# Two 64-column operands side by side for the level scores and the router, and slots counted by token halves

## What is computed

```python
def step(state, xs):                      # chunks of the recurrence, four heads
    qc, kc, vc, gc = xs
    b = jnp.cumsum(gc, axis=-2)
    diff = b[:, :, :, None, :] - b[:, :, None, :, :]
    decay = jnp.exp(jnp.where(causal[:, :, None], diff, -jnp.inf))
    scores = jnp.einsum('bhtk,bhsk,bhtsk->bhts', qc, kc, decay)
...
def hierarchical_moe(h, w_rg, w_re, w_gate, w_up, w_down):
    g_logits = (t @ w_rg).astype(F32)     # 4 groups
    e_logits = (t @ w_re)...              # 16 experts, those of the best group are kept
    top_v, top_i = lax.top_k(e_in, TOP_K_IN_GROUP)
    act = (jax.nn.silu(hg) * hu * gates[..., None])
    y = jnp.einsum('nef,efd->nd', act, w_down)
```

## Time and profile before

| what | value |
|---|---|
| median of 3 runs | 1021.76 us (1020.68 to 1021.91) |
| the profiled execution | 1021.73 us, of which the span is 1019.8 us |
| PE busy | 999.2 us (98%) |
| PE weight loads busy | 547.1 us (54%) |
| DVE busy | 477.2 us (47%) |
| ACT, POOL busy | 136.4 us, 98.8 us |
| read from HBM | 283.33 MB |
| products of the levels (L715) | 256 matmuls in the trace, 31.2 us |
| products of the router (L926) | 64 matmuls, 7.5 us |

### The profile page before, as it was taken

One profiled execution on the slowest core, in us unless ns is written; L12 is line 12 of the kernel. 1 busy time (PEld: TensorE's weight loads), 2 busy tenths in 40 slices (PEclk: granted clock), 3 DMA queues, 4 the chain that ended last, 5 costly groups with the idle time before them and its releaser, 6 DMA issues.

```text
span 1019.8 us, 11159 instructions
## 1 busy us (share of the span) xinstructions
PE 999.2 (98%) x4494; PEld 547.1 (54%) x4494; DVE 477.2 (47%) x814; ACT 136.4 (13%) x323; POOL 98.8 (10%) x123
## 2 busy tenths in 40 slices
PE   8999999999999999999999999999999999999996
PEld 7657555669575454333334855565975433333332
DVE  2533375766554224432444636566655544444424
ACT  2211000411010010101112000032120010111111
POOL 3051032000010000000000512210000100000000
PEclk9999999999999999999999999999999999999999
DMA  9973000963379999999999420067385799999995
GB/s 359 425 299 131 35 0 6 409 249 123 125 277 391 406 423 421 419 423 420 421 420 420 163 82 1 1 254 285 148 327 193 297 421 420 421 420 421 421 415 220
DMA packets 44826, 293.58 MB, mean 288 GB/s; under 512 B 5472, under 2 KB 5728, under 8 KB 13024
## 3 DMA queue, kind: packets, MB, share of 16 engines
q1 hardware_dynamic: 38000, 266.36, 64.3%
q10 hardware_dynamic: 5616, 22.24, 5.6%
q0 software_dynamic: 1152, 4.19, 1.1%
HBM read 283.33 MB, written 9.44 MB: 287 GB/s over the span
## 4 chain that ended last, share of the span: by engine, by line
PE 89%; SPq 5%; DMA 3%; DVE 2%; issue 1%; POOL 0%; ACT 0%; DVEq 0%; POOLq 0%
PE bank L1001 18%; PE bank L1075 10%; PE bank L590 8%; PE bank L620 6%; PE bank L789 5%; PE bank L622 5%; PE bank L600 5%; PE bank L843 5%; PE bank L907 5%; SPq L512 5%; PE bank L693 5%; PE bank L1036 5%; PE bank L715 3%; DMA ring<-in_w_experts 3%; PE bank L580 2%; PE bank L877 1%
## 5 line engine op out<-in xcount | busy, mean ns | idle before, releaser
L1001 PE MATMUL bank<-ring,hT 128*64 128x512 f32 x704 | 195.0, 593 | 0.0
L1001 PEld LDWEIGHTS bank<-ring,hT 128*64 128x64 f32 x704 | 62.5, 137 | 87.2 <-issue 86.9
L590 PE MATMUL bank<-ring,hT 128*128 128x512 f32 x192 | 84.4, 592 | 0.0
L1937 DVE TENSOR_TENSOR x<-bank,x 128x512 f32<-128x512 f32 x64 | 44.3, 692 | 54.5 <-PE bank L1036 54.5
L1955 DVE TENSOR_SCALAR xs<-xs 128x512 f32<-128x512 f32 x8 | 3.4, 426 | 124.0 <-ACT xs L1315 124.0
L1036 PE MATMUL bank<-PT 128*128 128x512 f32 x128 | 59.2, 605 | 0.0
L1075 PE MATMUL bank<-ring,Vx 128*64 128x512 f32 x160 | 57.1, 596 | 1.4 <-DMA ring<-in_w_experts 1.3
L590 PEld LDWEIGHTS bank<-ring,hT 128*128 128x128 f32 x192 | 35.6, 190 | 40.2 <-issue 40.2
L1075 PE MATMUL bank<-ring,xs 128*64 128x512 f32 x224 | 56.7, 595 | 0.0
L600 PE MATMUL bank<-hT,ring 128*128 128x256 f32 x256 | 55.7, 379 | 0.8 <-DVE hT L1586 0.8
L789 PE MATMUL bank<-ring,hT 128*128 128x512 f32 x128 | 56.3, 595 | 0.1
(11 more groups left out here) (296 smaller groups left out, 1559.2 us busy)
## 6 DMA issues: line engine op xcount, KB each, us to landing
ring<-in_w_experts SPq DMA_DIRECT2D x146, 1024.0 KB, 15.0
ring<-in_w_mix SPq DMA_DIRECT2D x60, 1024.0 KB, 14.5
work<-in_w_experts SPq DMA_DIRECT2D x20, 1024.0 KB, 12.7
late<-in_w_experts SPq DMA_DIRECT2D x10, 1024.0 KB, 18.1
late<-in_w_mix ACTq DMA_DIRECT2D x4, 2048.0 KB, 10.0
keys<-in_w_experts SPq DMA_DIRECT2D x8, 1024.0 KB, 21.9
rot<-by_slot ACTq DMA_DIRECT2D x14, 512.0 KB, 8.0
by_slot<-late ACTq DMA_DIRECT2D x1, 4096.0 KB, 38.3
```

The costliest lines, as they stand in the source:

```text
L590: last = nc.tensor.matmul(b[:, :], lhs[:, c, m * P:(m + 1) * P], w[:, c, :], start=(c == 0), stop=(c == C - 1))
L1001: last = nc.tensor.matmul(banks[2 + g][b2 * CAP:(b2 + 1) * CAP, :], rows_T_of(p)[:, c, b2 * CAP:(b2 + 1) * CAP], w, start=(c == 0), stop=( ...
```

## The change

It has four parts.

1. **Levels 1 to 6 in 64-key parts** (`HALF`, `QUARTER`, `later`). The 64 keys of each half of a block become a stationary operand of 64 columns, two of them side by side in a bank, and only the later queries of each pair at that level, 32 of 64 columns, are the moving operand. DVE copies from half the partitions at a time, under a mask, 4 x 32 elements in each. **Level 7** (`TOP`) is one 64 x 64 product for each head and block, the two blocks side by side, and is copied without a mask. Level 0 stays.
2. **Router** `logits`: 64 tokens as the stationary operand, two such side by side.
3. **Router by token halves**: block 0 gets its own job `rank0`, its slots are made while block 1 is on its way, and its `hot` tile too (`first_hot(0)`, semaphore `r_first`). PE gathers by block: `gather(0, c2)` runs before and after the job "rank", `gather(1, c2)` after the last `hot`. Block 1's slots count down from the top of an expert (`top16`), so that its count needs nothing of block 0. One `keep_busy` product stands before "rank" and one after it, where there were two and two.
4. **The wait for the scatter** (`r_sent`) and the loads of the rows of pairs 1 and 2 move on ACT from ahead of the pairs' loop into pair 0: the wait stands ahead of the first exponential, behind `units_read(0, "gate")`, and the loads behind it.

```diff
@@ PE, levels
+                    if j == TOP:
+                        pe.wait_ge(q_done, 16 * L + 2 * j)
+                        pe.wait_ge(k_done, 14 * L + 2 * (j - 1))
+                        tops = [open_bank(L, f"lev{j}_{m}") for m in range(M)]
+                        for a in range(HG_HEADS):
+                            for m, b in enumerate(tops):
+                                last = nc.tensor.matmul(b[HALF * m:HALF * (m + 1), a * HALF:(a + 1) * HALF], K[:, a, m * P:m * P + HALF],
+                                                        Q[:, a, m * P + HALF:(m + 1) * P], start=True, stop=True)
...
-                            last = nc.tensor.matmul(b[:, a * P:(a + 1) * P], K[:, a, m * P:(m + 1) * P],
-                                                    Q[:, a, m * P:(m + 1) * P], start=True, stop=True)
+                            for i in range(2):
+                                if j:
+                                    last = nc.tensor.matmul(b[HALF * i:HALF * (i + 1), a * QUARTER:(a + 1) * QUARTER], K[:, a, m * P + HALF * i:m * P + HALF * (i + 1)],
+                                                            later(Q[:, a, m * P + HALF * i:m * P + HALF * (i + 1)], j), start=True, stop=True)
@@ PE, router
-                        last = nc.tensor.matmul(b[:, 0:NR], hT[:, c, m * P:(m + 1) * P], router[:, c, :], start=(c == 0), stop=(c == C - 1))
+                        for i in range(2):
+                            part = slice(HALF * i, HALF * (i + 1))
+                            last = nc.tensor.matmul(b[part, 0:NR], hT[:, c, m * P + HALF * i:m * P + HALF * (i + 1)], router[:, c, :],
+                                                    start=(c == 0), stop=(c == C - 1))
...
-                p_seventh("p_3")
+                NE = N_EXPERTS
+                p_seventh("p_3", range(3))
+                pe.wait_ge(chosen_done, 2 * L + 1)
+                b = open_bank(L, "rank0")
+                close(nc.tensor.matmul(b[:, 0:NE], before[:, :], chosen[:, 0, :], start=True, stop=True))
+                p_seventh("p_3", range(3, 4))
@@ ACT
-                def first_loads():
-                    act.wait_ge(r_sent[L], 16 * 2 * M)
-                    for p in (1, 2):
-                        load_rows(p)
...
                     units_read(p, "gate")
+                    if p == 0:
+                        act.wait_ge(r_sent[L], 16 * 2 * M)
                     nc.scalar.activation(rexp_of[L], banks[2][:, :], ACT.Exp, scale=-1.0).then_inc(r_gexp[L], 1)
+                    if p == 0:
+                        for q in (1, 2):
+                            load_rows(q)
@@ DVE, levels
+                        if j == TOP:
+                            emptied(V.tensor_copy(S[0:HALF, m, :, HALF:P], found[HALF * m:HALF * (m + 1), 0:HG_HEADS * HALF].rearrange("p (a t) -> p a t", t=HALF)))
+                        elif j:
+                            h = 1 << (j - 1)
+                            for i in range(2):
+                                rows, cols = slice(HALF * i, HALF * (i + 1)), slice(HALF * i, HALF * (i + 1))
+                                into = S[rows, m, :, cols].rearrange("p a (b u i) -> p a b u i", u=2, i=h)[:, :, :, 1, :]
...
+                                copied = V.copy_predicated(into, mask, found[rows, 0:HG_HEADS * QUARTER].rearrange("p (a b i) -> p a b i", a=HG_HEADS, i=h))
@@ DVE, router
                 choose(0)
+                scale_tile(L, 2, 0)
+                wait_job(dve, L, "rank0")
+                emptied(V.tensor_tensor(rank[:, 0, :], base16, bank("rank0")[:, 0:N_EXPERTS], ALU.add))
                 p_sum("p_3", (1, 1))
...
+                wait_emptied(dve, L, "rank0")
+                slots(0)
                 wait_emptied(dve, L, "p_3")
                 rows_T("t5", 1, 24)
-                for m in range(M):
-                    scale_tile(L, 2, m)
+                scale_tile(L, 2, 1)
+                first_hot(0, r_first[L])
                 choose(1)
```

More of the change, by code:

```diff
@@ L75, in job_list @@
     jobs += [(f"p_{i}", "D") for i in (7, 6, 5, 4)]
-    jobs += [("t5_00", "D"), ("t5_01", "D"), ("p_2", "D"), ("rt0", "D"), ("p_3", "D"), ("t5_10", "D"), ("t5_11", "D"), ("rt1", "D")]
+    jobs += [("t5_00", "D"), ("t5_01", "D"), ("p_2", "D"), ("rt0", "D"), ("rank0", "D"), ("p_3", "D"), ("t5_10", "D"), ("t5_11", "D"), ("rt1", "D")]
     return jobs + [("rank", "D")]
@@ L398, in wait_free, with later @@
                 wait_job(eng, l, LAST_USE[old])
+        def later(view, j):
+            h = 1 << (j - 1)
+            return view.rearrange("p (b u i) -> p b u i", u=2, i=h)[:, :, 1, :]
         def shares_to(k):
@@ L936, in layers_from, with gather @@
                 logits(0)
-                p_seventh("p_3")
+                NE = N_EXPERTS
[4 more added lines that the diff above has]
+                p_seventh("p_3", range(3, 4))
+                def gather(m, c2):
+                    b = banks[FIRST_ROWS[c2]]
+                    for k in range(4):
+                        last = nc.tensor.matmul(b[:, k * P:(k + 1) * P], xs[:, m, (4 * c2 + k) * P:(4 * c2 + k + 1) * P], hot[:, m, :],
+                                                start=(m == 0 and k == 0), stop=(m == 1 and k == 3), skip_group_check=True)
+                    return last
                 def router_kv(i, chunks=range(C)):
@@ L952, in layers_from, with keep_busy @@
                 logits(1)
-                def keep_busy(n):
+                def keep_busy():
                     if L + 1 == DEPTH:
[L957 to L962, removed]
+                        wait_emptied(pe, L, BANK_BEFORE["router_kv0"])
+                        nc.tensor.matmul(banks[BANK["router_kv0"]][:, :], ident[:, :], hT[:, 0:2, :], start=True, stop=True)
                 router_kv(0, range(2, 6))
+                pe.wait_ge(normed, 6 * L + 5)
+                pe.wait_ge(r_first[L], 1)
+                gather(0, 0)
+                keep_busy()
                 pe.wait_ge(chosen_done, 2 * L + 2)
                 b = open_bank(L, "rank")
[L966 to L971, removed]
+                nc.tensor.matmul(b[:, 0:NE], before[:, :], chosen[:, 1, :], start=True, stop=True)
+                nc.tensor.matmul(b[:, NE:2 * NE], ones[:, :], chosen[:, 0, :], start=True, stop=False)
+                close(nc.tensor.matmul(b[:, NE:2 * NE], ones[:, :], chosen[:, 1, :], start=False, stop=True))
+                gather(0, 1)
+                keep_busy()
                 router_kv(0, range(6, C))
                 router_kv(1)
-                keep_busy(2)
                 def fill(p, s, quarters=range(4)):
@@ L1011, in layers_from @@
                 for c2 in range(2):
-                    for k in range(4):
-                        for m in range(M):
-                            cols = xs[:, m, (4 * c2 + k) * P:(4 * c2 + k + 1) * P]
-                            last = nc.tensor.matmul(banks[FIRST_ROWS[c2]][:, k * P:(k + 1) * P], cols, hot[:, m, :], start=(m == 0), stop=(m == M - 1))
-                    routed_job(last)
+                    routed_job(gather(1, c2))
                 if L + 1 < DEPTH:
```

48 lines of the change are left out of this document (30 added, 18 removed).

## The result

The changed kernel takes 1015.22 us (median of 10 runs, 1013.02 to 1018.96 apart from one execution of 1294.68 us at a mean clock of 0.75, which the comparison leaves out). The kernel before took 1021.84 us in 10 runs beside it. The ratio is 0.9937, with a 95% interval of 0.9924 to 0.9951: faster by 0.6%. That is 3.7 us above the forecast of 1011.5, inside the range of 1005.5 to 1018.5 and above the forecast's own narrower one (1008.5 to 1014). The profiled execution took 1015.30 us, its span is 1013.4 us, so 6.4 less than before. Its other nine runs spread with the mean granted clock: three spans of 1011.1 to 1011.9 us at 0.994 to 0.995, three of 1013.3 to 1013.4 at 0.993 to 0.994, three of 1016.6 to 1017.1 at 0.989 to 0.991.

A forecast was written before the change was run, and what follows sets the result against it. PE's own work was taken to bound each layer's first three quarters, PE and DMA nearly level at layer 1's end. 8.5 + 0.7 + 2.5 - 1.4 + 0 = 10.3 us off 1021.8 gave 1011.5, range 1005.5 to 1018.5.

The forecast's parts named there:

- Levels, 8.5 us: Levels 1 to 7: half-width loads in pairs, less switch costs, save 4.23 us a layer, 8.5 us in both.
- sign of 1.25 us: Expected in the trace: 1.25 us from a level's first matmul to the next projection, the level's matmuls taking 0.9.
- wider pairs: Levels and logits: four short instructions need 0.073 us instead of 0.055, 4.9 us less gained, 1016.4 us; chance 0.16.
- no overlap: Levels and logits: loads of two halves run one after another, 0.111 us a pair, 1026.5 us, slower; chance 0.10.
- Router in layer 0, 0.7 us: Layer 0's router: two logits save 0.46 us each, less about 0.1 waiting for chosen and 0.1 for an extra product.
- Router in layer 1, 2.5 us: Layer 1's router: shorter logits, DVE chain and gather start gate_up earlier by 1.2 to 3.7 us, taken as 2.5.
- the middle of the three cases: Layer 1's router: clock at half until the count, then full, so gate_up starts at 797.0 us.
- Row loads in layer 0, 1.4 us: Layer 0's experts: pair 1's rows land late, a new PE wait of 1.3 to 2.6 us, taken as 1.4 lost.
- The scatter in layer 1: Layer 1's experts: the exponential waits for the scatter, bounds 0 to 2.6 us, taken as 1.0 lost.
- bounds of +1.3 and -2.7: Layer 1's expert phase: 1.3 us regained, 0.5 lost to rows, 1.0 to the exponential, about 0 within these bounds.
- The regained wait, 1.3 us: End of layer 1: DMA starts 2.4 us earlier, so PE's 1.3 us wait for a weight should go.
- given back at the end: End of layer 1: DMA is full, so an earlier PE only waits for weights; no change, 1021.8 us; chance 0.05.

The follow-up runs named there:

- experiment 5: Kernel before with only the levels in 64-key parts, nothing of the router: 1013.49 us, ratio 0.9918.
- experiment 6: Kernel before with only the levels in 64-key parts, both parts of a pair writing output partitions 0 to 63: 1023.97 us, ratio 1.0029.
- experiment 7: Kernel before with only the router's logits in 64-token parts: 1019.05 us, ratio 0.9976.
- experiment 1: Changed kernel with the scatter wait and the row loads of pairs 1 and 2 back ahead of the pairs' loop: 1011.70 us, ratio 0.9896.
- experiment 4: Kernel before with only the scatter wait and row loads moved into pair 0, in both layers: 1024.92 us, ratio 1.0033.
- experiment 3: Changed kernel with layer 0's scatter wait and two row loads right behind the half job, ahead of the gate's: 1010.82 us, ratio 0.9889.
- experiment 2: Changed kernel, but in layer 1 pair 0's exponential runs ahead of the scatter wait and only the row loads wait: 1014.28 us, ratio 0.9921.
- experiment 8: Changed kernel with block 0 scattered once its slots are counted, the overflow branch removed, wait and row loads behind the half job in both layers: 1009.06 us, ratio 0.9876.

## Why the prediction came out as it did

**Levels, 8.5 us: right in size and cause.** Forecast were 0.90 + 0.15 in and 0.19 out; the trace has 1.06 for the level and 7.06 for the projection behind it, 6.87 elsewhere. (The forecast's sign of 1.25 us from a level's start to the next projection counts the way out, 0.19, a second time; its own sum has 1.05.) Experiment 5 has the sum alone (8.4), experiment 6 the cause. The rivals of wider pairs and of no overlap are out: 1.06/16 is 0.066 us for a pair with the switch in it. By the time alone, wider pairs (1016.4) would have looked nearer than the forecast. The case of about 62 ns for each matmul that the prediction cited from the Trainium skill, "TensorE: Matmul & The Clock Gate", section "Wait — 56ns, not 53.3ns?", is told there of matmuls with hardware decode switched off. It would make a pair 0.124 us, so this kernel isn't in that case. (The forecast read from the earlier trace rows that PE alone bounds the first three quarters of each layer. DMA is full from 357 us on in layer 0, which ends at 562, and from 806 to 816 on in layer 1, so it is nearer two thirds and somewhat over half; the levels and the router lie ahead of both.)

**Router in layer 0, 0.7 us: nearly right.** In the changed kernel the way from the first matmul of `logits(0)` to `gate_up` is 24.7 us instead of 25.7, 1.0 less. The forecast's parts were 0.9 for part 2 and -0.2 for part 3; by experiment 7 part 2 alone gives 1.2, so part 3 costs about 0.2.

**Router in layer 1, 2.5 us: right, on a clock that varies by as much as 1.1 us.** The way is 16.7 us instead of 19.2. The clock fell as it did in the earlier trace rows, here around 785 (0.62 over 784 to 788), which was the middle of the three cases that the forecast weighed. In experiment 1 it did not fall and the way is 1.1 us shorter. With the router of before the way is 19.0 to 19.2 us in two profiles and 20.3 in two others (experiments 4 and 5), by the clock too, so that the number could have come out a microsecond off either way.

**Row loads in layer 0, 1.4 us: mis-sized.** The step "I take 1.4 us lost, since most landings are nearer to 8" took the median over the row loads of both layers. In the kernel before the one that went out at 327.5 us, nearest to this place, took 9.1. These two take 9.22 us to land in the changed kernel and 8.65 in experiment 4; PE waits 2.55 and 2.0, `gate_up` and the wait 16.50 us instead of 13.88. The upper bound, 2.6, was the right reading.

**The scatter in layer 1: this step failed.** The forecast said "I take 1.0" for the exponential, with a bound of 2.6. The gate's columns were through at 791.09 + 7.1 = 798.2 us and the exponential ran at 801.58, 3.4 us late. The scatter needs longer beside SP's loads. From POOL's last issue to what waited for all four it is:

| kernel | last issue | SP's first load behind it | scatter through behind it |
|---|---|---|---|
| before | 799.87 | held back, 5.8 | 4.9 |
| experiment 1 | 790.52 | held back, 5.7 | 4.8 |
| experiment 3 | 790.17 | 1.6 | 7.2 |
| changed kernel | 793.51 | 1.3 | 8.0 |
| experiment 2 | 793.35 | 1.3 | 8.0 |
| experiment 8 | 786.01 | 5.0 | 6.2 |

Experiment 1 and the changed kernel differ by part 4 alone: SP's loads at 1.3 us instead of 5.7 come with 3.2 us more for the scatter. Experiment 8 suggests that it isn't SP's loads alone: its scatter of block 0 was still on its way when block 1's was issued, and block 1's took 6.2. The forecast had the collision, as a bound, but gave the late exponential 1.0 and took the row loads' wait as 0.5, apart from it. In fact they add up along one chain: 3.4 late, then 7.87 for the rows. PE waited 2.30 and 1.14 us.

**What the stall does to the clock was in no term.** From the end of the first of these two waits PE ran at the lower level for some 7 us. The eight transposes of the rows took 1.97 us where layer 0's took 1.09, and `down` 1.22 more. So from `gate_up` to the end of `down` layer 1 lost 5.6 us where 1.5 were priced. Together with the regained 3.45 the phase comes to -2.2 us, within the forecast's bounds of +1.3 and -2.7 and far from its 0.

**The regained wait, 1.3 us: the number right for another reason, and mis-sized.** The term was to come from DMA's earlier start. The profile's list of waits showed 1.3 us; the two jobs' own lengths (9.87 and 7.62 against 7.02) would have shown 3.45. And with little or no delay of PE the earlier start regains 0.3 us (experiment 4) or 1.15 (experiment 8). In the changed kernel 3.45 came back because PE itself was 5.6 us later: weights were no longer what came last. From the start of layer 1's `gate_up` to the end of the span it is 216.7 us in every profile of this table, to 0.1 us, plus the last two columns:

| kernel | SP's first load behind the start of `gate_up` | PE's stall up to the end of `down` | waits for weights at the end |
|---|---|---|---|
| before | 6.0 | 0 | 3.45 |
| experiment 5 | 5.9 | 0 | 3.15 |
| experiment 1 | 8.1 | 0 | 5.4 |
| experiment 4 | 3.7 | 0.45 | 3.2 |
| experiment 8 | 3.7 | 0 | 2.3 |
| experiment 3 | 3.7 | 3.9 | 0 |
| changed kernel | 3.7 | 5.6 | 0 |

So the rival "given back at the end" holds in part. Part 3 brings `gate_up` forward by more than the scatter (POOL's last issue stands 2.4 us behind the start of `gate_up` in experiment 1, and 0.2 before), and while SP's loads wait for the scatter, 2.0 us of the gain go into waits for weights. Part 4 cures that and puts a stall of about the same size in its place, 5.6 against 5.4. Its price by the spans is therefore layer 0's 2.6 and hardly anything in layer 1's experts; the rest of the 3.2 is the router's clock, less 0.7 us by which `logits(0)` of layer 0 started later in experiment 1.

Along the chain the spans' difference is made of 3.9 (levels of layer 0), 1.0 (its router), -2.7 (its rows), 4.0 and 2.4 (levels and router of layer 1), -5.6 and 3.45: 6.4 us, as found. The 3.9 us that the forecast had too much are 2.2 in layer 1's experts, 1.3 in layer 0's rows and 0.6 in the levels, less 0.2 in the routers. The levels give 7.9 there instead of 8.4 to 8.5 because the start of `logits(0)` in layer 0 lies between 281.5 and 282.9 us among kernels with the same levels; what makes it was not looked into.

**Left open.** Why the last `down` of experiment 4 waits 1 us longer than before, and whether the scatter's delay comes from sharing the DMA engines or from its place behind loads on each of them: no run here tells these apart. Nor does any run show what makes the clock fall at layer 1's router in some kernels and not in others.

## What to carry to other kernels

Two operands of half width pay only when they go to different halves, and each change of the form costs, so count pairs against switches. Before a wait is moved, follow the chain through everything that it then stands in front of, transfers too, and price transfers at what they take beside the traffic that the move itself lets loose. Where the end is bound by weights, a stall ahead of it is refunded in part and a gain is taken back in part: read the lengths of the last jobs, not only the list of waits, and put the fix where the engine is the bound, here layer 0.

## What was not expected of the hardware

A form of 64 columns is paid by the columns: 0.057 us for one load and its matmul behind another of the same half (experiment 6), 0.111 for one of 128 columns, and 0.057 for two of different halves (experiment 5), with 0.15 us for the way in and 0.19 for the way out. An indirect scatter of 2 MB that was through 4.8 us behind its last issue took 7.2 to 8.0 when loads of 1 MB started 1.3 to 1.6 us behind that issue. And in layer 1 the clock was at the lower level for some 7 us where PE had waited 2.3 and then 1.1 us, some 1 us apart (changed kernel), and where it had waited 0.6 and then 2.9 (experiment 2). It was so for some 3 us with waits of 1.2 and 1.6 (experiment 3). A single wait of 2.0 to 2.6 us at the same place of layer 0 was not followed by it: the transposes behind it took 1.09 us.
